# Stage openings of a 20-stage float32 network: where the remainder products of the first four K tiles stand for the upper 128 tokens

## The reference, cut to what matters

```python
# first block, for each of 4 layers (mixers a, b, c, a)
x = x + 0.5 * rms_norm(swiglu_ffn(rms_norm(x, g[0]), ffn_w_gate_up[i, 0], ffn_w_down[i, 0]), g[1])
h = rms_norm(x, g[2])
x = x + rms_norm(mixer(h), g[3])                      # every mixer starts with h @ w_in
x = x + 0.5 * rms_norm(swiglu_ffn(rms_norm(x, g[4]), ffn_w_gate_up[i, 1], ffn_w_down[i, 1]), g[5])
# second block, for each of 4 layers (mixers nsa, stick, conv, moba)
x = x + mixer(_rms_norm(x, attn_norm[i]))             # starts with h @ w_in as well
x = x + jnp.square(jax.nn.relu(_rms_norm(x, mlp_norm[i]) @ mlp_w_up[i])) @ mlp_w_down[i]
```

## Time and profile before

| | us |
|---|---|
| median of 3 runs | 3565.32 |
| lowest, highest | 3556.3, 3566.18 |
| profiled execution, whole | 3553.03 |
| profiled execution, span of its instructions | 3551.3 |
| PE matmul busy | 3339.0 (94%) |
| PE weight load busy | 2890.8 (81%) |
| DVE busy | 1992.6 (56%) |
| ACT busy | 1644.4 (46%) |
| mean granted TensorE clock | 0.970 |

### The profile page before, as it was taken

How to read it: one execution, slowest core, us unless ns; L and a number is a source line. 1 busy time by engine, 2 the same in 40 slices (tenths; PEclk the granted TensorE clock), 3 DMA queues, 4 the chain that set the end, 5 groups by cost and what they waited for, 6 DMA issues and landing times.

```text
span 3551.3 us, 52163 instructions
## 1 busy us (share of the span) xinstructions
PE 3339.0 (94%) x19516; PEld 2890.8 (81%) x19516; DVE 1992.6 (56%) x2832; ACT 1644.4 (46%) x2477; POOL 202.2 (6%) x239
## 2 busy tenths in 40 slices
PE   7998999998999998999998999799969998999899
PEld 6976988976988977988977988688758877887697
DVE  5555556566556555656555655655555555556563
ACT  4444444444444445444443543544444446445553
POOL 1011000000000000001001011000000000001100
PEclk9998999998999999999998998899989999999999
DMA  6553555642655543555552655045514550555254
GB/s 200 188 181 97 183 178 185 193 149 79 190 182 185 187 140 107 172 189 177 187 187 77 196 175 167 13 160 184 178 48 166 187 168 1 168 194 178 78 190 154
DMA packets 399915, 551.98 MB, mean 155 GB/s; under 512 B 34960, under 2 KB 235744, under 8 KB 399744
## 3 DMA queue, kind: packets, MB, share of 16 engines
q1 hardware_dynamic: 395936, 536.10, 46.6%
q0 software_dynamic: 2976, 10.81, 0.9%
q10 hardware_dynamic: 832, 2.74, 0.2%
HBM read 548.47 MB, written 1.05 MB: 155 GB/s over the span
## 4 chain that ended last, share of the span: by engine, by line
PE 80%; DVE 11%; ACT 3%; DMA 2%; issue 1%; SPq 1%; POOL 0%; DVEq 0%; ACTq 0%; POOLq 0%
PE G L720 14%; PE G L724 14%; PE G L721 14%; PE G L812 10%; PE G L814 10%; PE G L813 10%; DVE ring_lo_sb L1696 4%; PE T L696 2%; PE G L1181 1%; PE O L935 1%; PE S L906 1%; ACT ring_hi_sb L1252 1%; DVE act_hi_sb L1710 1%; SPq L507 1%; DVE act_lo_sb L1720 1%
## 5 line engine op out<-in xcount | busy, mean ns | idle before, releaser
L1696 DVE TENSOR_TENSOR ring_lo_sb<-ring_sb,ring_hi_sb 128x1024 fp32r<-128x1024 f32 (+2 forms) x996 | 1203.6, 1224 | 693.8 <-ACT ring_hi_sb L1252 673.6
L1252 ACT ACTIVATE ring_hi_sb<-ring_sb 128x1024 fp32r<-128x1024 f32 (+1 forms) x1028 | 1060.6, 1044 | 858.9 <-DMA ring_sb<-ffn_w_down 222.6
L812 PE MATMUL G<-act_hi_sb,ring_hi_sb 128*128 128x256 f32 x3072 | 861.9, 281 | 2.7 <-DVE ring_lo_sb L1696 2.3
L813 PE MATMUL G<-act_lo_sb,ring_hi_sb 128*128 128x256 f32 x3072 | 856.6, 279 | 0.0
L814 PE MATMUL G<-act_hi_sb,ring_lo_sb 128*128 128x256 f32 x3072 | 856.3, 279 | 0.0
L720 PE MATMUL G<-ring_hi_sb,hid_hi_sb 128*128 128x512 f32 x1456 | 583.4, 401 | 13.9 <-DVE hid_lo_sb L1729 8.1
L812 PEld LDWEIGHTS G<-act_hi_sb,ring_hi_sb 128*128 128x128 f32 x3072 | 576.9, 188 | 6.0 <-DVE ring_lo_sb L1696 5.7
L721 PE MATMUL G<-ring_lo_sb,hid_hi_sb 128*128 128x512 f32 x1456 | 581.0, 399 | 0.0
L814 PEld LDWEIGHTS G<-act_hi_sb,ring_lo_sb 128*128 128x128 f32 x3072 | 577.2, 188 | 0.0
L813 PEld LDWEIGHTS G<-act_lo_sb,ring_hi_sb 128*128 128x128 f32 x3072 | 576.0, 187 | 0.0
L724 PE MATMUL G<-ring_hi_sb,hid_lo_sb 128*128 128x512 f32 x1408 | 559.3, 397 | 0.0
(11 more groups left out here) (230 smaller groups left out, 2560.2 us busy)
## 6 DMA issues: line engine op xcount, KB each, us to landing
ring_sb<-ffn_w_gate_up SPq DMA_DIRECT2D x704, 256.0 KB, 3.9
ring_sb<-ffn_w_down SPq DMA_DIRECT2D x352, 256.0 KB, 3.7
ring_sb<-mlp_w_up SPq DMA_DIRECT2D x256, 256.0 KB, 3.8
ring_sb<-mlp_w_down SPq DMA_DIRECT2D x256, 256.0 KB, 3.6
ring_sb<-a_w_in SPq DMA_DIRECT2D x48, 256.0 KB, 4.2
ring_sb<-sb_w_in SPq DMA_DIRECT2D x48, 256.0 KB, 3.9
ring_sb<-moba_w_in SPq DMA_DIRECT2D x48, 256.0 KB, 3.9
ring_sb<-nsa_w_in SPq DMA_DIRECT2D x40, 256.0 KB, 3.9
```

Source lines behind the costliest of these rows:

```text
L812: mm(dst, hi, act_hi[:, kt, :], start=(kt == 0 and f == 0), stop=False, skip_group_check=True)
L813: mm(dst, hi, act_lo[:, kt, :], start=False, stop=False, skip_group_check=True)
L1252: fn(ring_hi[:, s_, :, 0:w], ring[:, s_, :, 0:w], ACT.Copy).then_inc(hi_ready, 1)
L1696: v.tensor_tensor(ring_lo[:, s_, :, 0:w], ring[:, s_, :, 0:w], ring_hi[:, s_, :, 0:w], ALU.subtract).then_inc(lo_ready, 1)
```

## The change

In an opening, for t = 1 and chunk 0 alone, the order of the products changes. Before: 16 products with `act_hi` (the second eight behind a wait for `act_hi` of group b = 1), a wait for both groups of `act_lo`, 8 remainder products. After: 8 products with `act_hi` (units 0 and 1), a wait for `act_lo` of b = 0, the 4 remainder products of units 0 and 1 (with the two `unit_used` increments), a wait for `act_hi` of b = 1, 8 products with `act_hi` (units 2 and 3), a wait for `act_lo` of b = 1, the last 4 remainder products (with the other two increments). For t = 0 nothing changes. The number of matmuls, waits and increments is the same, and each K tile still gets its three products.

```diff
+                half = CHUNK_UNITS // 2
+
+                def remainders(first, end):
+                    for kt in range(UNIT_K * first, UNIT_K * end):
+                        last = lo_product(dst, lhs, kt, ts, (n + kt // UNIT_K) % RING, kt % UNIT_K, width,
+                                          kt == KT - 1)
+                        if t == TT - 1 and kt % UNIT_K == UNIT_K - 1:
+                            last.then_inc(unit_used, 1)
+                    return last
                 for u in range(CHUNK_UNITS):
                     slot = (n + u) % RING
                     if t == 0:
                         unit_split(n + u, step, i)
-                    if lo_later and u == CHUNK_UNITS // 2:
+                    if lo_later and u == half:
+                        if t == TT - 1:
+                            copied(c["T"] - 2)
+                            remainders(0, half)
                         pe.wait_ge(act_hi_in, c["act_hi"])
...
                 if lo_later:
-                    copied(c["T"] - 2)
+                    if t == 0:
+                        copied(c["T"] - 2)
                     copied(c["T"] - 1)
-                    for kt in range(KT):
-                        last = lo_product(dst, lhs, kt, ts, (n + kt // UNIT_K) % RING, kt % UNIT_K, width,
-                                          kt == KT - 1)
-                        if t == TT - 1 and kt % UNIT_K == UNIT_K - 1:
-                            last.then_inc(unit_used, 1)
+                    last = remainders(0 if t == 0 else half, CHUNK_UNITS)
```

## The result

| | before | after |
|---|---|---|
| median, us (11 runs each, measured by turns) | 3556.3 | 3539.32 |
| lowest, highest | 3545.49, 3566.18 | 3529.57, 3551.8 |
| ratio after / before, 95% interval | | 0.9949 [0.9933, 0.9965] |
| profiled execution, whole | 3553.03 | 3529.59 |
| its span | 3551.3 | 3527.9 |

The change made the kernel faster by 0.51%, between 0.35 and 0.67%. The median of before, too, is 9.0 us lower in these eleven runs than in the three that the forecast started from, so of the 15.3 us between forecast and result 9.0 belong to the starting value and 6.3 to the gain, 17.0 us instead of 10.7.

What follows compares the result with a forecast made beforehand. PE bounds the kernel (80% of the chain), stalled behind openings by late-started transfers. Stalls of 5.7 + 5.6 - 0.4 = 10.9 us, 0.2 left for rests, give -10.7: 3565.32 - 10.7 = 3554.6 us, range 3543 to 3567.

Steps and rivals of the forecast that it cites:

- The release: Openings, upper half: units 0 and 1 are given free 8 products earlier, 1.87 us; units 2 and 3 stay.
- The transfers follow: Behind the openings: ffn issues all move 1.87 us, mixers' from unit 10 about 1.3; DMA share above 0.3 instead of 0.05.
- the 1.3 to 1.87 that the prediction took as bounds: Units behind the opening: their landings move earlier by 1.3 us at least and 1.87 at most.
- The stalls: Weight-load waits on late units, in chunk 2 of ffn stages (5.7 us) and five plain mixers (5.6 us), go.
- the 0.2 us that I left for rests: Allowance for stalls left over; conv's largest sum is within 0.2 us of the 1.3 us bound.
- The moved wait: Ninth product of t = 1: earlier wait for act_lo costs 0, with margins 0.39 us to product, 0.16 to weight load.
- The bound of 2 us: Upper cost of the moved wait: a 0.10 us restart in each of 20 openings, 2.0 us.
- so the whole stage moves with PE: Behind chunk 2: later loads and DVE work come earlier too, so a stage keeps what it gains.
- Given back in part: Rival: units 10 and 11 move by half of 1.87 us or a stage's end waits; about -5.5 us, chance 0.20.
- only units 8 and 9: Rival: only these land earlier, so stalls go in three of thirteen stages; about -1.4 us, chance 0.08.
- slower: Rival: early act_lo wait stalls PE at the ninth product of t = 1; +6.9 us, 3572 us, chance 0.05.
- no effect: Rival: SP waits for something other than unit 0, so the release is in vain; 0 us, chance 0.05.

Runs made afterwards that it cites:

- Experiment 3: The changed kernel's product order, but units 0 and 1 given free as before, with the 18th and 20th product; ratio to the kernel before 0.9995.
- experiments 4 to 8 and 10: Changed kernel: loop written out (4, 0.9933); transposes added (5), moved (6, 3537.84 us), one added (7, 0.9969); products added (8, 3554.74, 3548.4 us); loop written out, mlp transposes parted (10, 0.993).
- experiments 1, 3 and 7: Old release: kernel before unchanged (1.0004); new product order with old release (0.9995); kernel before with one more transpose ahead of chunks 2 and 3 (1.0001).
- experiment 7: One more transpose per group ahead of chunks 2 and 3, in both kernels; ratios to the unchanged kernel before 1.0001 (before) and 0.9969 (after).
- experiment 2: The changed kernel once more, without an edit, for a second profile; ratio to the kernel before 0.9937, median 3532.09 us.

## Why the prediction was right and wrong

**The release** was right to the hundredth: forecast 1.87 us earlier, measured 1.88, and 1.86 to 1.88 in all 20 openings. Experiment 3 shows that it is the cause, and that the order of the products alone is not.

**The transfers follow.** Right: DMA share 0.35 in the stretch where it was 0.05, and forecast above 0.3. In the fourth opening SP waited for nothing, and in six of the eight ffn stages every issue for units 8 to 11 moved by 1.86 to 1.88 us as forecast; in the other two the later ones moved by 1.4 and 1.6. In the mixers the issues from unit 10 on moved by 0.8 to 1.6 us, about 1.0 in five of the eight, where 1.3 had been worked out. The landings of these units moved by 0.9 to 2.9 us, wider on both sides than the 1.3 to 1.87 that the prediction took as bounds. That conv's stalls were gone in this profile (its landings moved by 1.9 us and more, its later issues by 0.9) was luck in part: in eight later profiles with the early release 0.3 to 1.4 us of them are left.

**The stalls.** Right in place and in kind: the waits of L812 went from 5.7 us to nothing, those of the five plain mixers too; the 0.2 us that I left for rests was 0 in both profiles of after and 0.3 to 1.4 us in the nine altered ones with the early release (experiments 4 to 8 and 10), in seven of them in conv, where the prediction had seen the least margin. In mix_c the wait stayed, 1.4 us, as argued. In mix_b the one of 0.6 us stayed and the second, 0.3 us, is gone, but it is missing in the profiles of experiments 1, 3 and 7 too, which release late. The size was read from one execution: 10.7 us in the sum, while four profiles with the old release have 11.3, 15.2, 10.7 and 12.8 us, 12.5 in the mean. Between the two kernels of experiment 7 the gain was 12.8 us.

**The moved wait** cost nothing, as argued from the 0.16 us of margin to the weight load: idle time before L724 at the new place is 0, and the load runs 0.23 us ahead of its product. The bound of 2 us wasn't used. The Trainium skill (TensorE: Matmul & The Clock Gate, Step-by-step: what each phase is for) says that weight loads are pulled ahead of running matmuls; by that rule the trace agrees, with 551.08 for the load and 551.31 for its product.

**What failed** is the step "so the whole stage moves with PE". It lets a stage gain its stall and no more, and so puts the pace of the products behind the opening at nothing, with "12 products of 0.117" as a constant. (That the 24 products of the opening keep their 0.234 us and cost nothing was right.) The 0.117 us is one of two values, 117.8 and 113.3 ns, taken at a group of transposes for the rest of a stage, and the earlier trace rows show only the slow one. The rows that would have told it were there: windows with 172 and with 179 matmuls in the trace of before, in stages that do the same work. Between the two profiles the paces are worth 10.8 us, nearly as much as the stalls; in the mean of many executions, by the shares above, some 6 us, which is an estimate and hangs on the link that is not shown. The term for the stalls was too small by 1.8 us besides (12.5 in the mean, 10.7 in the sum). That gives 12.5 + 6.3 = 18.8 us, beside mean gains of 17.6 us in the first measurement and 23.7 in experiment 2. The remaining 9.0 us of the 15.3 between forecast and result are no part of the mechanism: they are the starting value, a median of three runs.

**The rivals.** None held. Given back in part and only units 8 and 9 are out, since the stalls at units 10 and 11 went too; slower is out by the unchanged 9.6 us on `act_lo`; no effect by the ratio. All of them asked how much of 10.7 us would remain. None asked what besides could come. For a result faster by more than 0.3%, which is what came, the prediction gave 0.38, less than the 0.58 for one within. The terms named for the range, half the gain (5.4), the restarts (2) and half the spread (5), lead from 3554.6 to its upper end, 3567. The lower end, 3543, lies about as far on the other side, though only the half spread of the three points that way, and even so it was missed, by the 9.0 us of the starting value and the 6.3 of the gain together. Of the three runs behind it the lowest, 3556.3, was the one at the later median.

**What stays open:** whether an unstalled stage takes the fast pace more often at all, and if so why; whether it does in the old order; and what the pace depends on in the chip.

## What to carry to other kernels

When a buffer is given free by the last of several products, look at which of them could be done sooner: here four products pulled forward by eight places let a resting transfer stream start 1.9 us earlier in each of 20 openings, and a stall of about 1 us vanished in thirteen of them, at no cost. Before summing up waits, compare the pace of stages that do equal work, by counting instructions in equal windows without gaps; if there are two paces, a comparison of one execution of each kernel mixes the change with a draw, and both the size of a stall and the pace need several profiles. Where a mechanism of less than 0.5% is to be measured, hold the other one fixed in both kernels, see in more than one profile that it is held, and measure the pair.

## What was unexpected of the hardware

**Two paces at one granted clock.** Products of 256 columns with a weight load each ran at 117.8 or at 113.3 ns start to start, at a granted clock of 1.00 (2.4 GHz) either way, for some 90 us at a time, over the eight chunks behind chunk 2 without a change, across loop turns, transfers and ACT's and DVE's work. In stages without stalls the pace changed only at a group of transposes between such products. With 4 or 6 in the group ahead of chunk 3 up to three quarters of the ffn stages went on fast, with 5 or 7 none of 32 (4 profiles), with 8 no mlp stage, and with 4 behind one or two added products none of 16. The group ahead of chunk 2 has 4 transposes too, and behind it all ffn stages of before and after began slow. A start behind a stall in chunk 2 could change the pace as well: in before the last 60 of its 96 products ran at 113 ns in two ffn stages, and so did the last 60 or more in five stages of later profiles. All seven were slow behind the next transposes.

The step across the group of transposes tells the pace behind it. From the last product of chunk 2 to the first behind the transposes it was 472 to 474 ns in every ffn stage that went on fast (35) and 475 to 478 ns in every one that did not (53), over the eleven profiles with 4 transposes there and nothing added (nanosecond starts of the trace's records). In after that is 472 to 474 against 477 ns, some 4 ns, the size of the difference in pace. The value of 475 ns was seen in 14 stages, all of them with a wait in chunk 2 (0.2 us or more) and all slow. What these steps stand for no run here shows.

For the same products the Trainium skill (TensorE: Matmul & The Clock Gate, Back-to-back issue gap) gives columns / 2.4 GHz + 2.5 ns for a matmul alone, which is 109 ns for 256 columns and 216 for 512, and says that in a stream with weight loads both operations set the spacing, with a measured 131 ns for 512 columns. Here, in such a stream of fp32r operands, it was 113.3 or 117.8 ns and 233 ns. That is near the first figures and far from the 131; the measurement decides.
